# Differential attention: the values step as 24 split products of 512 columns at the end of a head, with ten residual blocks kept in DRAM meanwhile

## What is computed

```python
def diff_attend(q, k, v, pos, lam):      # 8 heads, q and k of 2 x 128, v of 256
        sc = jnp.einsum('bhcqd,bhckd->bhcqk', qi, k_t).astype(jnp.float32) * scale
        dist = jnp.abs(pi[:, :, None] - pos[:, None, :]).astype(jnp.float32)
        sc = sc + (-slopes[None, :, None, None] * dist[:, None])[:, :, None]
        sc = jnp.where(chunk_allowed(pi, pos)[:, None, None], sc, -jnp.inf)
        p = jax.nn.softmax(sc, axis=-1)
        p_diff = p[:, :, 0] - lam * p[:, :, 1]
        return jnp.einsum('bhqk,bhkd->bhqd', p_diff.astype(v_t.dtype), v_t)

def diff_layer(x, ...):
    z = rms_norm(x, norm_g) @ w_in
    q, k, v, gate = jnp.split(z, [B_QK, 2 * B_QK, 2 * B_QK + B_WIDTH], axis=-1)
    ...
    o = rms_norm(diff_attend(q, k, v, pos, lam), subln_g) * (1.0 - lam_init)
    return x + (o * jax.nn.silu(gate)) @ w_out
```

## Time and profile before

| | |
|---|---|
| time, median of 3 runs | 3152.26 us (3150.14 to 3152.27) |
| the profiled execution: its time, its span | 3148.18 us, 3146.3 us |
| TensorE (PE) busy | 3096.2 us, 98% of the span |
| VectorE (DVE) busy | 1543.7 us, 49% |
| ScalarE (ACT) busy | 792.3 us, 25% |
| GpSimd (POOL) busy | 2067.2 us, 66% |
| granted TensorE clock, mean | 0.995 |
| eight attention stretches, first scores of each to the last V | 2171.0 to 2975.7 us |

### The profile page before, as it was taken

The page is one execution under the profiler, slowest core; times in us unless marked ns, Lnnn a source line. Parts: engine busy times, 40 slices in busy tenths (PEclk is TensorE's granted clock), DMA queues, the critical chain, the costliest instruction groups (busy, mean ns, idle before and its releaser), DMA issues.

```text
span 3146.3 us, 59089 instructions
## 1 busy us (share of the span) xinstructions
PE 3096.2 (98%) x19586; PEld 2476.2 (79%) x19586; DVE 1543.7 (49%) x3018; ACT 792.3 (25%) x1532; POOL 2067.2 (66%) x3460
## 2 busy tenths in 40 slices
PE   8999999999999998999999999999999999999999
PEld 6777777788888786788778778888888788888787
DVE  4565555566565756612566675144244324423600
ACT  2333333243333202200244452021112112211300
POOL 7555545588787795987634436887666666666575
PEclk9999999999999998999999999999999999999999
DMA  5222221232222232333211112332222222222142
GB/s 159 62 62 62 62 61 56 62 92 80 80 79 75 68 94 69 87 93 93 75 40 33 47 40 76 95 95 81 81 77 69 87 73 77 77 80 80 54 127 87
DMA packets 461249, 239.55 MB, mean 76 GB/s; under 512 B 27917, under 2 KB 456392, under 8 KB 461128
## 3 DMA queue, kind: packets, MB, share of 16 engines
q1 hardware_dynamic: 457148, 232.14, 25.4%
q10 hardware_dynamic: 3980, 5.63, 0.5%
HBM read 233.52 MB, written 4.19 MB: 76 GB/s over the span
## 4 chain that ended last, share of the span: by engine, by line
PE 92%; DVE 5%; issue 1%; ACT 1%; DMA 1%; POOL 0%; SPq 0%; DVEq 0%; ACTq 0%; PEldq 0%; POOLq 0%
PE proj L341 25%; PE proj L342 24%; PE proj L343 24%; PE work L2547 2%; PE work L2142 2%; PE work L341 1%; PE work L343 1%; PE work L2135 1%; PE work L342 1%; PE work L721 1%; PE work L1281 1%; PE work L735 1%; PE work L1510 1%; PE work L1524 1%; DVE lat_sq L1795 0%
## 5 line engine op out<-in xcount | busy, mean ns | idle before, releaser
L317 POOL TENSOR_SCALAR w_hi<-raw_weights 128x256 fp32r<-128x256 f32 x1728 | 743.6, 458 | 1056.0 <-DMA raw_weights<-w_in 352.5
L321 POOL TENSOR_TENSOR w_lo<-raw_weights,w_hi 128x256 fp32r<-128x256 f32 x1728 | 1341.8, 809 | 0.0
L341 PE MATMUL proj<-x_hi,w_hi 128*128 128x512 f32 x2976 | 1219.1, 410 | 12.3 <-DVE x_lo L1781 8.7
L342 PE MATMUL proj<-x_lo,w_hi 128*128 128x512 f32 x2976 | 1177.5, 396 | 0.0
L343 PE MATMUL proj<-x_hi,w_lo 128*128 128x512 f32 x2976 | 1177.1, 396 | 0.0
L341 PEld LDWEIGHTS proj<-x_hi,w_hi 128*128 128x128 f32 x2976 | 559.9, 188 | 160.4 <-issue 23.6
L343 PEld LDWEIGHTS proj<-x_hi,w_lo 128*128 128x128 f32 x2976 | 559.0, 188 | 136.7
L342 PEld LDWEIGHTS proj<-x_lo,w_hi 128*128 128x128 f32 x2976 | 560.7, 188 | 118.8 <-issue 2.2
L341 PE MATMUL proj<-o_hi,w_hi 128*128 128x512 f32 x256 | 103.4, 404 | 3.9 <-DVE o_lo L1167 3.2
L342 PE MATMUL proj<-o_lo,w_hi 128*128 128x512 f32 x256 | 101.8, 398 | 0.0
L343 PE MATMUL proj<-o_hi,w_lo 128*128 128x512 f32 x256 | 101.8, 398 | 0.0
(11 more groups left out here) (485 smaller groups left out, 3908.6 us busy)
## 6 DMA issues: line engine op xcount, KB each, us to landing
raw_weights<-w_in SPq DMA_DIRECT2D x260, 256.0 KB, 3.1
raw_weights<-b_w_in SPq DMA_DIRECT2D x256, 256.0 KB, 3.0
raw_weights<-a_w_in SPq DMA_DIRECT2D x100, 256.0 KB, 3.1
raw_weights<-w_out SPq DMA_DIRECT2D x64, 256.0 KB, 3.1
raw_weights<-a_w_out SPq DMA_DIRECT2D x64, 256.0 KB, 3.1
raw_weights<-b_w_out SPq DMA_DIRECT2D x64, 256.0 KB, 3.1
raw_weights<-a_w_kv_up SPq DMA_DIRECT2D x32, 256.0 KB, 2.8
mix<-x SPq DMA_DIRECT2D x4, 1024.0 KB, 8.8
```

The costliest lines, as they stand in the source:

```text
L317: pool.tensor_scalar(part(hi_v, s, q), part(raw_v, s, q), 1.0, 1.0, ALU.mult, ALU.mult).then_inc(hi_done, 1)
L321: pool.tensor_tensor(part(lo_v, s, q), part(raw_v, s, q), part(hi_v, s, q).bitcast(F32), ALU.subtract).then_inc(w_split, 1)
L341: pe.matmul(out, w_h, a_h, start=start, stop=False)
L342: pe.matmul(out, w_h, a_l, start=False, stop=False)
```

## The change

It does the following, and nothing outside the differential stage and the last stage's additions:
1. **V moves and changes form.** The V of each block is dropped. All four blocks' transposed probabilities are kept (`d_pt_hi`, `d_pt_lo`), and once per head, behind T3 and two `yield 1`, 24 matmuls of 512 columns (two halves x four blocks of keys x three products) make the result.
2. **Low parts.** pT now writes the high part; VectorE gets a new step pl (PSUM minus high part) for each block and vl0, vl1 for the values.
3. **Order.** pl of block k-1 stands behind nbb of block k in VectorE's list. T of block k needs pl of block k-1 (before: pT).
4. **Tail of a head.** ScalarE's four copies o go; it squares the two PSUM banks directly (osq0, osq1). VectorE weighs (`og`) ahead of and behind oadd, and multiplies by the norm (`o`) at the end; yields around the sums are 2 and 4 (before 1 and 4).
5. **Residual.** The kept probabilities lie over blocks 6 to 15 of `mix`. ScalarE stores these (128 x 5120 floats, 2560 KB) to DRAM at the start of the stage and loads them back after the last head; VectorE and ScalarE wait for the store before head 0, VectorE waits for the load behind the first four additions of the last stage.

The diff, cut to its core:

```diff
+        KEPT = range(6, KB)
+        kept_at = o_start + 4 * SEQ * KEPT[0]
+        d_pt_hi, d_pt_lo = (tokens(a11.over(f"diff_probs_keys_{x}", kept_at + 4 * TB * SEQ * n, TB * SEQ, F32R)[:, :], SEQ)
+                            for n, x in enumerate(("hi", "lo")))
+        d_vt_lo = a11.over("diff_v_tok_lo", kept_at + 8 * TB * SEQ, 2 * SEQ, F32R)
+        h_kept = nc.dram_tensor("h_kept", (P, len(KEPT) * SEQ), F32).ap()
...
-        dpipe = range(TB + 2)
+        dpipe = range(TB + 1)
...
-        DI_ACT = steps("diff_act", "sq0 sq1 sq2 sq3 rows vt0 vt1 hq0 hq1 t0 hk0 hk1 t1 " + dpiped("ea{0} eb{0}", "pT{0}", "o{0}").replace(" o1", " o1 osq0") + " osq1")
+        DI_ACT = steps("diff_act", "sq0 sq1 sq2 sq3 rows vt0 vt1 hq0 hq1 t0 hk0 hk1 t1 " + dpiped("ea{0} eb{0}", "pT{0}", "") + " osq0 osq1")
+        DI_DVE = steps("diff_dve", "ms " + RSQRT + " nsl lq0 lq1 vl0 vl1 gate0 k0 k1 lk0 lk1 gate1 " +
+                       " ".join((f"rec{k - 1} rl{k - 1} pb{k - 1} p{k - 1} " if k else "") +
+                                (f"sca{k} mxa{k} nba{k} scb{k} mxb{k} nbb{k} " if k < TB else "") +
+                                (f"pl{k - 1}" if k else "") for k in range(TB + 1)) +
+                       " og0 oadd og1 oms " + tagged("o_") + " o0 o1")
...
                 if 1 <= k <= TB:
                     need(DI_DVE, f"p{k - 1}")
                     if k >= 2:
-                        need(DI_ACT, f"pT{k - 2}")
+                        need(DI_DVE, f"pl{k - 2}")
...
-                if k >= 2:
-                    need(DI_ACT, f"pT{k - 2}")
-                    if k >= 3:
-                        need(DI_ACT, f"o{k - 3}")
-                    for x in range(2):
-                        for c in range(TB):
-                            mm = pe.matmul(work[3][:, x * P:(x + 1) * P], d_vt[:, 256 * c + x * P:256 * c + (x + 1) * P],
-                                           d_pt[:, c * P:(c + 1) * P], start=(c == 0), stop=(c == TB - 1))
-                    mm.then_inc(DI_PE.mark(f"V{k - 2}"), 1)
-                    yield 1
             yield 1
-            need(DI_DVE, "oadd1")
-            token_sums(pe, work[2], d_sq[0], lambda b: b).then_inc(DI_PE.mark("osum"), 1)
+            need(DI_DVE, f"pl{TB - 1}")
+            for x in range(2):
+                for c in range(TB):
+                    vs = slice(256 * c + x * P, 256 * c + (x + 1) * P)
+                    mm = multiply(pe, work[3 - x], d_vt_hi[:, vs], d_vt_lo[:, vs], d_pt_hi[:, c], d_pt_lo[:, c],
+                                  c == 0, c == TB - 1)
+                mm.then_inc(DI_PE.mark(f"V{x}"), 1)
+            yield 2
+            need(DI_DVE, "oadd")
+            token_sums(pe, work[0], d_sq[0], lambda b: b).then_inc(DI_PE.mark("osum"), 1)
...
+            act.dma_start(h_kept, mix[:, KEPT[0] * SEQ:]).then_inc(h_stored, 16)
             pos = io["positions_2"]
             act.dma_start(d_pos_i[:, :], pos.to_broadcast([P, SEQ])).then_inc(dpos_loaded, 16)
...
+                if k >= 1:
+                    need(DI_ACT, f"pT{k - 1}")
+                    ks = slice((k - 1) * P, k * P)
+                    done(dve.tensor_tensor(d_pt_lo[:, :, ks], tokens(work[2][:, :], P), d_pt_hi[:, :, ks].bitcast(F32),
+                                           ALU.subtract), f"pl{k - 1}")
```

More of the change, by code:

```diff
@@ L2406, in build @@
         dk_hi = [a11.take(f"diff_k_hi{c}", SEQ, F32R) for c in range(2)]
+        d_vt_at = a11.at
         d_vt = a11.take("diff_v_tok", 2 * SEQ)
+        d_vt_hi = a11.over("diff_v_tok_hi", d_vt_at, 2 * SEQ, F32R)
         dist = tokens(a11.take("distances", TB * SEQ)[:, :], SEQ)
@@ L2442, in build @@
         dpos_loaded = sem("dpos_loaded")
[L2443 to L2447 removed]
+        DI_PE = steps("diff_pe", "rows sums vt0 vt1 inv0 inv1 " + dpiped("Sa{0} Sb{0}", "T{0}", "") + " V0 V1 osum oinv")
+        DI_ACT = steps("diff_act", "sq0 sq1 sq2 sq3 rows vt0 vt1 hq0 hq1 t0 hk0 hk1 t1 " + dpiped("ea{0} eb{0}", "pT{0}", "") + " osq0 osq1")
[4 more added lines that the diff above has]
+                       " og0 oadd og1 oms " + tagged("o_") + " o0 o1")
         OUT3 = OutStage("out3", 9, U_OUT3, T_OUT3, mix2_v, xh, xl)
@@ L2618, in diff_heads_act @@
                     need(DI_PE, f"T{k - 1}")
[L2619 to L2631, removed]
+                    act.activation(d_pt_hi[:, :, (k - 1) * P:k * P], tokens(work[2][:, :], P), ACT.Copy)\
+                       .then_inc(DI_ACT.mark(f"pT{k - 1}"), 1)
+            for x in range(2):
+                need(DI_PE, f"V{x}")
+                act.activation(d_sq[x][:, :], work[3 - x][:, :], ACT.Square).then_inc(DI_ACT.mark(f"osq{x}"), 1)
         def diff_dve(dve):
@@ L2709, in diff_heads_dve @@
                 low(c, dq_lo, d_q, dq_hi, "q")
+            for x in range(2):
+                need(DI_ACT, f"vt{x}")
+                by_block = lambda v: tokens(v[:, :], 256)[:, :, x * P:(x + 1) * P]
+                done(dve.tensor_tensor(by_block(d_vt_lo), tokens(work[x][:, :], P), by_block(d_vt_hi).bitcast(F32),
+                                       ALU.subtract), f"vl{x}")
             take_gate(0)
@@ L2745, in diff_heads_dve, with weigh @@
                                                       rs[:, 4 * c + k:4 * c + k + 1], ALU.mult, ALU.mult), f"nb{x}{k}")
-            behind_scores()
[L2748 to L2751, removed]
+                if k >= 1:
[3 more added lines that the diff above has]
+                                           ALU.subtract), f"pl{k - 1}")
+            def weigh(x):
+                done(dve.scalar_tensor_tensor(gate(x), gate(x), sub_gain[:, x:x + 1], work[3 - x][:, :],
+                                              ALU.mult, ALU.mult), f"og{x}")
+            behind_scores()
+            need(DI_ACT, "osq0")
+            weigh(0)
+            need(DI_ACT, "osq1")
+            done(dve.tensor_tensor(d_sq[0][:, :], d_sq[0][:, :], d_sq[1][:, :], ALU.add), "oadd")
+            weigh(1)
             need(DI_PE, "osum")
             chain()
-            done(dve.tensor_scalar(work[2][:, 16:20], work[2][:, 0:4], 1.0 / B_V, EPS, ALU.mult, ALU.add), "oms")
-            rsqrt(dve, DI_DVE, p, work[2][:, 16:24], d_small[:, 64:68], d_small[:, 72:76], d_small[:, 68:72], "o_")
+            done(dve.tensor_scalar(work[0][:, 16:20], work[0][:, 0:4], 1.0 / B_V, EPS, ALU.mult, ALU.add), "oms")
+            rsqrt(dve, DI_DVE, p, work[0][:, 16:24], d_small[:, 64:68], d_small[:, 72:76], d_small[:, 68:72], "o_")
             need(DI_PE, "oinv")
             for x in range(2):
-                done(dve.scalar_tensor_tensor(gate(x), gate(x), sub_gain[:, x:x + 1], work[3][:, :],
-                                              ALU.mult, ALU.mult), f"og{x}")
-                chain()
-                done(dve.tensor_tensor(gate(x), gate(x), d_v[:, x * SEQ:(x + 1) * SEQ], ALU.mult), f"o{x}")
+                done(dve.tensor_tensor(gate(x), gate(x), work[1][:, :], ALU.mult), f"o{x}")
         OT_PE = steps("out_turn_pe", "t0 t1 t2 t3")
@@ L2807, in out3_dve @@
             out_split_dve(dve, OUT3, range(AHEAD3[-1][1], KB))
-            with dve.Fori(0, KB // 4) as i:
+            for j in range(4):
+                add_tile(dve, OUT3, 0, j, y_group)
+            dve.wait_ge(h_back, 16)
+            with dve.Fori(1, KB // 4) as i:
                 dve.wait_ge(OT_PE.sem, OT_PE.after(i))
```

12 lines of the change are left out of this document (8 added, 4 removed).

## The result

The changed kernel takes 3201.42 us (median of 4 runs, 3196.95 to 3203.80) where the kernel before takes 3152.2 us on the same chip (3150.14 to 3152.27): ratio 1.016, 95% interval 1.0148 to 1.0172. It is slower by 49 us, as forecast in sign and inside the range; the forecast was +62. The profiled execution took 3202.64 us with a span of 3200.8.

What follows compares the result with a forecast made beforehand. TensorE, busy 98% of the span, was taken as the bound. Seven heads at 7.5 - 1.54 + 1.5 give 52.2, the last 9.7: +62 us on the profiled 3148.2; with 4.1 to the median, 3214 us, range 3190 to 3232.

Steps and rivals of the forecast that it cites:

- pl: end of nbb to rec: VectorE's gap between nbb and rec, each block: pl stands there and makes rec 1.17 us later, accumulating.
- waits, heads 0 to 6: TensorE's waits at T2 and T3 in a head: 1.0 and 6.9 us, 7.5 remaining after the relief.
- relief: While TensorE stands, GpSimd runs out of weights to split, so VectorE's longest steps may shorten: 0.4 us a head off.
- V: V as 24 products of 512 columns at 0.234 us, 5.61 us a head instead of 7.15: saves 1.54 us.
- the clock: TensorE's granted clock falls to half behind the T3 stand; eight products at 0.19 us extra: 1.5 us a head.
- last head to the end: Last head: ScalarE's splitting of output operands delays pl three times, waits 11.0 us; 9.7 us in sum.
- store: Store of 2560 KB at the stage's start: 22 us, hidden with two microseconds of margin, costing nothing.
- the walk through the fourth head: Steps of VectorE and TensorE followed block by block in the fourth head: T1 no wait, 7.9 us of waits in all.
- p2 takes 2.86 us as p3 did: VectorE from rec2 to the end of p2 in the fourth head: taken as 2.86 us, the length p3 had before.
- VectorE runs fast: Rival: while GpSimd stands, p takes 2.1 us in every block, up to 2.2 us a head less, 3197; chance 0.10.
- V and its parts (5.0 us): TensorE between T2 and T3: this work no longer lies there, given as one of two causes of the 7.9 us wait.
- The first rival: Waits stand, but the clock doesn't fall or is back before TensorE works again: 12 us less, 3202; chance 0.15.

Runs made afterwards that it cites:

- The first experiment: Changed kernel with eight more parts of the projection ahead of T3 in heads 0 to 6, last head unchanged: 3147.07 us, ratio 0.9992 to the kernel before.
- the fourth: Kernel before the change with only the store of ten `mix` blocks, the load back and their waits added: 3151.13 us, ratio 1.0001.
- the second: Changed kernel with transposes going to two PSUM banks in turn and pl one block later in VectorE's list: 3178.75 us, ratio 1.0091.
- third: Changed kernel with V at the head's end as 8 plain float32 matmuls, without pl, vl or low parts: 3192.32 us, ratio 1.0134.
- the last experiment: Two-bank kernel with GpSimd making weights' low parts by a one-operand multiply (the light GpSimd; wrong results): 3132.96 us in one run, against 3178.75.
- both mends: Changed kernel with transposes in two banks, eight parts ahead of T3 in heads 0 to 6, two in the last: 3139.98 us, ratio 0.9969.

## Why the prediction was right, and where its terms were off

The mechanism was right: T3 waits in each of eight heads for the last step of p, VectorE is late because pl stands between nbb and rec, the clock falls behind the stand, and the store is hidden. The first experiment takes the wait away and the loss with it; the fourth clears the transfers; the second and third separate the two causes of the wait. The forecast was 13 us too high. By its terms:

| term | forecast | measured |
|---|---|---|
| pl: end of nbb to rec | 2.24 us | 2.18 us |
| waits, heads 0 to 6 | 7.5 us a head (T2 1.0, T3 6.9, relief 0.4) | 5.5 (T2 0, T3 5.5) |
| V | -1.54 | -1.73 |
| the clock | +1.5 | about +2.2, worked out below |
| a head | +7.46 | +6.0 |
| last head to the end | +9.7, with waits of 11.0 | +6.4, with waits of 8.3 |
| store | 22 us, hidden | 9.3 us, hidden |

The range was met with some luck: a wait 2.0 us a head too long stood against a clock 0.7 us too cheap, and 13 us remained of the two and the last head.

**The wait (the walk through the fourth head) is the mis-sized term.** Its steps for pl were right to 0.06 us. What failed is "p2 takes 2.86 us as p3 did", and the same for p3. In the kernel before GpSimd is busy throughout such a phase; the window from rec3 to the end of p3 (columns as in rows 1, the fifth engine is GpSimd):

```profile
2526.40:2529.20 2.80, 2.80 (x21) 2.54 (x20) 2.69 (x4) 0.00 (x0) 2.80 (x5) 1.00 0.00 0
```

And in the changed kernel, the phase that T3 waits for:

```profile
2553.28:2554.95 1.67, 0.00 (x0) 0.00 (x0) 1.56 (x4) 0.00 (x0) 0.00 (x0) 0.75 0.00 0
```

GpSimd 2.80 of 2.80 us busy there, 0.00 of 1.67 here; VectorE's four instructions take 1.56 us where they took 2.69. The delay moves the phase out of GpSimd's work. The two phases ahead of it, from rec1 and rec2, lie between:

```profile
2536.61:2539.31 2.70, 2.70 (x13) 2.16 (x12) 2.60 (x4) 0.00 (x0) 1.64 (x3) 1.00 0.16 43
2544.96:2547.19 2.23, 2.23 (x11) 1.78 (x10) 2.13 (x4) 0.00 (x0) 0.91 (x2) 1.00 0.42 124
```

The forecast took 0.4 us a head off for this and gave the rest to a rival of 0.10 ("VectorE runs fast", up to 2.2 us a head less). In size this rival is what came: p3 is 1.2 us shorter than walked, p2 0.6 (in the other heads 0.8 to 1.2) and p1 0.2, which took the wait at T2 away and brought 7.9 us down to 5.65. Its reason isn't what the runs show. The prediction reasoned that TensorE stands and so stops GpSimd. But with cover ahead of T3 and no stand (first experiment) the same phase is as short, and with V at the end in plain float32 (third) TensorE stands through the whole phase and GpSimd works on, and it is as long as before:

```profile
2526.70:2528.36 1.66, 1.64 (x8) 0.97 (x6) 1.55 (x4) 0.00 (x0) 0.20 (x1) 1.00 0.38 114
2543.44:2546.26 2.82, 0.00 (x0) 0.00 (x0) 2.71 (x4) 0.36 (x1) 2.82 (x5) 0.71 0.00 0
```

It is when the phase falls. The clearest evidence that GpSimd sets this length is the last experiment.

One number beside the walk is misread, without touching the sum: "V and its parts (5.0 us)" is the whole distance from T2 to T3 of before. What went out there is 3.2 us, and as much between T1 and T2.

The Trainium skill has the reason on its page "SBUF — State Buffer", section "Who interferes with whom": VectorE's second pair of ports into SBUF is shared with GpSimd. A VectorE instruction with two inputs in SBUF contends with a GpSimd instruction that reads SBUF, and so does one such as a tensor_scalar when it runs in a mode of two ports; one with a single input there and the other in PSUM does not. The rows agree: p reads two from SBUF, 1016 against 755 ns; the scaling is a tensor_scalar, 904 against 544; pl reads one from PSUM, and took 0.69 us with the full GpSimd at every place shown above. Who pays depends in these traces on the GpSimd instruction. Beside the subtraction of two operands p takes 1.03 to 1.12 us in the kernel before. Beside one of one operand, which reads SBUF too, p keeps 0.75 to 0.77 us in the light kernel, and the GpSimd instruction that begins during p takes up to 0.90 us instead of 0.40.

**The clock** was charged too low. The heads of the changed kernel are 106.96 us (the pitch with both mends, nothing waiting) plus the wait plus what the clock takes: for index 1, 114.23 - 5.50 - 106.96 = 1.8 us; for index 3, 115.52 - 5.65 - 106.96 = 2.9. The half clock lasts 3.41 us in some heads and 6.83 in others, and the prediction had one length from one place. On the mean, 6.0 - 5.5 + 1.73 = 2.2 us. This can be read from the traces directly. In the fourth head the half clock begins while TensorE still stands:

```profile
2554.11:2560.94 6.83, 5.86 (x16) 4.80 (x17) 1.50 (x3) 0.60 (x1) 0.00 (x0) 0.50 0.10 30
```

T3 starts at 2555.09, so 5.85 of the 6.83 us lie behind the stand, and half of them, 2.9, is the price found above. Over the seven heads 4.4 us on the mean lie behind the stand, half of which is 2.2. The first rival, no fall, didn't come in this kernel, but it did in one head of the kernel with two banks, behind a stand of 2.51 us.

**V** was costed at 0.234 us a product, the distance within scores; it took 0.228, 5.47 us a head in place of 5.61, which is most of the difference between 1.54 and 1.73. The 131 ns of the Trainium skill ("TensorE: Matmul & The Clock Gate", section "Back-to-back issue gap"), from which the prediction estimated a saving of 4.0 us a head, aren't seen in this form in any run here.

**The last head**: waits of 8.3 us instead of 11.0 (T1 0.53, T2 0.79, T3 6.98). ScalarE's splitting delays pl as reasoned, and by as much. VectorE, the block that T3 waits for:

```profile
3013.49 0.43 DVE L2754 SCALAR_TENSOR_TENSOR diff_rows<-diff_rows,diff_small 128x1 f32<-128x1 f32 x1
3016.41 0.69 DVE L2760 TENSOR_TENSOR diff_probs_keys_lo<-work,diff_probs_keys_hi 128x512 fp32r<-128x512 f32 x1 [2.49 <-ACT diff_probs_keys_hi L2631]
3017.21 0.17 DVE L2733 RECIPROCAL diff_rows<-diff_rows 128x2 f32<-128x2 f32 x1
...
3018.20 0.75 DVE L2741 SCALAR_TENSOR_TENSOR diff_probs<-diff_exp,diff_rows,diff_exp 128x512 f32<-128x512 f32 x1
```

From the end of nbb to rec it is 3.29 us where the other heads have 2.18, in each of three blocks: 3.3 us against the 3.1 that were added. What is too long is again the phase from rec to the end of p: it takes 2.63, 1.74 and 1.74 us, walked as 2.86 each, 2.5 us less in all. The sum as measured: waits +8.3; before, TensorE waited 2.3 us for `x_lo` (the larger one in the earlier trace rows) and 0.5 for a weight part, and after for neither, -2.8; V -1.7. That is 3.8 of the 6.4. The clock is at 0.50 from 3014.91 to 3021.74 us, but TensorE stands until 3019.01, so 2.7 us count and cost 1.4; the remaining 1.2 us stay unexplained.

**The store** of 2560 KB landed in 9.3 us, not 22 (in the changed kernel too, as the DMA view of its stage start shows):

```profile
h_kept<-mix ACTq DMA_DIRECT2D x1, 2560.0 KB, 9.3
diff_pos_int<-positions ACTq DMA_DIRECT2D x1, 256.0 KB, 10.4
```

One load of 1024 KB that shares the engines with three others, and with loads of weights, was a poor measure for one store. The load back took 9.0 us. Both were hidden either way, so the error moved nothing.

**What stays open.** What decides whether the half clock lasts 3.4 or 6.8 us, or doesn't come; and, within the 5.5 us of a head, exactly how much is the late pl and how much the lost cover, since each edit that moves one also moves p's phase with respect to GpSimd. The last head shows how far that goes: its waits at T are 8.3 us in the changed kernel, 1.0 with two banks and 2.9 with two banks and cover. The last head holds the rest of what could be had: with both mends it takes 218.3 us from its first score to the end, with the light GpSimd 210.0. With both mends it still stands 2.9 us at T3 and, right behind, 2.2 us for `x_lo`, and the clock falls; no run here goes after it.

## What to carry to other kernels

A step of TensorE that seems to be only work can be the cover for what comes next: before moving it, count the time between the two neighbours that remain, and compare it with the chain that feeds the second. If that chain is longer, the remedy is to move other work there; eight parts of projection at the right place turned 49 us of loss into nothing, and with the low parts moved one block later in VectorE's list into a gain of 11. And when an instruction's length is read from a trace, read with it what GpSimd was doing at that time: the same four instructions of VectorE took 1.6 us beside an idle GpSimd and 2.7 beside its subtractions.

## What the runs showed of the hardware

- TensorE's clock: behind every stand of 3.7 us and more in this stage the granted clock fell to 0.5 (for 3.4 or 6.8 us, part of it still in the stand); behind one of 2.51 us it stayed at 1.00, but it fell at 2970.2 us of the same kernel with only two stands of 0.8 us just before. The price in heads 0 to 6 was 1.6 to 3.0 us on top of the stand, within 0.3 us half of what of the low stretch lay behind the stand.
- GpSimd and VectorE: with GpSimd's subtraction of two operands VectorE's p took 1016 ns and the scaling 904; with a one-operand GpSimd instruction 755 and 544, and a one-operand GpSimd instruction that began during p took up to 0.90 us instead of 0.40.
- A store of 2560 KB from ScalarE's queue landed in 9.3 us, some 280 GB/s. The four 1024 KB loads of `x`, under way together, took 8.8 us each in the median.
